# Two attentions of a two-layer transformer block, weighed with their values as the stationary operand

## The chip, the cores and the metric

The kernel runs on one core of one Trainium2 chip. The metric is the device time of one execution in microseconds (us). Engines are named as the profile names them: PE is the matrix engine (PEld its weight loads), DVE the vector engine, ACT the scalar engine, POOL is GpSimd, SP the queue that issues most of the DMA transfers. A matmul has a stationary operand, which is loaded into the array, and a moving operand, whose columns stream through.

## The reference, cut to what matters

256 tokens of width 1024 pass a first block (grouped attention "a" with 8 query and 2 key/value heads of 64, differential attention "b", output projection, MLP) and a second one (gated FFN, an mLSTM and a "forgetting attention" of 16 heads of 64 side by side, gated merge, output projection, a second gated FFN). The change is about attention a and the forgetting attention (fox), whose two halves of eight heads are called fx0 and fx1:

```python
s = jnp.einsum('bkgqd,bksd->bkgqs', qblk, kt).astype(jnp.float32) * scale      # attention a
p = jax.nn.softmax(s, axis=-1)
return jnp.einsum('bkgqs,bksd->bkgqd', p.astype(vt.dtype), vt)

logits = jnp.einsum('bhqd,bhkd->bhqk', q_blk, k).astype(f32) * scale + (F_blk[..., :, None] - F[..., None, :])
logits = jnp.where(k_pos[None, :] <= q_pos[:, None], logits, -jnp.inf)          # fox
p = jax.nn.softmax(logits, axis=-1)
return jnp.einsum('bhqk,bhkd->bhqd', p.astype(v.dtype), v)
```

All is float32. Attention a's output goes into rows 0 to 511 of `w_out`, the fox output into `w_branch_b`.

## The kernel before, in words

**Large products.** Each weight matrix is streamed from HBM in units of 2x128 rows by 512 columns. ACT copies a unit into a rounded high part (L1525), DVE subtracts it for the low part (L1907), and PE forms high*high, high*low and low*high (L1217, L1221, L1222) for each of two token tiles, into one of two pairs of PSUM banks. The activations are the stationary operand and have to be there transposed and split in the same way: a group of four 128x128 transposes on PE into one PSUM bank, a copy into the high part on ACT, a subtraction for the low part on DVE.

**Attention.** Each attention works on rounds `i` of two heads and one tile of 128 queries: eight rounds in attention a and in each fox half, the first four for one tile of queries, the last four for the other. Two rounds are scored together: `scores` (L1293) issues four matmuls on the upper and the lower 64 rows of the array in turn (L1312). `soft` takes the maximum on DVE and the exponential with its row sums on ACT (L1680, L1685). The transposing step `turn` (L1332) turns the probabilities with up to four PE transposes (L1338) into a bank, ACT or DVE copies them to `PT`, and `weigh` (L1342) multiplies: the turned probabilities are stationary (128x128), the values move, 64 columns (L1357). The key blocks number two in attention a and in rounds 0 to 3 of fox, one in rounds 4 to 7 of fox because of the causal mask. PE does a float32 matmul as two instructions, so a round of `weigh` is 8 instructions, or 4 with one key block. The result has queries in partitions and 8x64 columns. After four rounds DVE inverts the row sums (L2184) and multiplies the bank by them into W1 (L2198 for a, L2189 for fox). Since the next product needs it transposed, PE turns it again: jobs `ta0`, `ta1` (one group of four transposes each, L1391) and `yb0`, `yb1` (two groups each, L1270), followed by the split on ACT and DVE. `yb` also waits until branch a's product has read yTh and yTl, which it overwrites, and fox may not write W1 before `yT` has read it. Differential attention b has the same shape but works with 128-column values (L1372) and is not changed.

**Order.** A planner (`plan`, L434) writes one list of steps which all engines follow. Large products come in fixed order, and after each half unit `tick` advances small jobs whose lag has run out; the lags stand in the table `LAG`, with `PACED` for blocks that tick several times per half unit, `ADA` for the pace of the modulation weights and `LO` for how late the low part of a unit is made. The five blocks of the first projection come as qb, kb, vb, qa, ka. Then nothing large is left but the output projection, whose blocks `ob` need attention b's result, and `oa` attention a's. In the meantime PE has only the small steps of the attentions. In the second block the fox attention runs beside the products o, ga, ba and gb, and `bb` needs its result.

POOL computes powers of small statistics (L2502), masks (L2546, L2552) and multiplies the mLSTM's gain (L2538).

Of the kernel before, what the change touches and what calls it, by code (L numbers as in the profile page):

```python
# [16 lines left out]
OUTS = 2  # L17
# [4 lines left out]
LAG = {("attn", "sums"): 5, ("attn_a", "wait"): 21, ("attn_as", "round"): 4, ("attn_as", "wait"): 0,  # L22
       ("attn_as", 0): 6, ("attn_as", 1): 4, ("attn_as", 2): 3, ("attn_as", 3): 12, ("attn_at", "round"): 8,
       ("attn_at", 0): 4, ("attn_at", 1): 5, ("attn_at", 2): 3, ("attn_at", 3): 3, ("attn_at", 4): 1,
       ("attn_at", 5): 10, ("attn_at", 6): 1, ("attn_at", 7): 17, ("attn_aw", "round"): 3, ("attn_aw", 0): 4,
       ("attn_aw", 1): 3, ("attn_aw", 2): 8, ("attn_aw", 3): 1, ("attn_aw", 4): 7, ("attn_aw", 5): 4,
       ("attn_aw", 6): 1, ("attn_aw", 7): 17, ("attn_b", "wait"): 2, ("attn_bm", "round"): 10, ("attn_bm", 0): 2,
       ("attn_bm", 1): 1, ("attn_bm", 2): 2, ("attn_bm", 3): 4, ("attn_bs", "round"): 4, ("attn_bs", "wait"): 0,
       ("attn_bs", 0): 4, ("attn_bs", 1): 4, ("attn_bs", 2): 4, ("attn_bs", 3): 4, ("attn_bt", "round"): 5,
       ("attn_bt", 0): 1, ("attn_bt", 1): 6, ("attn_bt", 2): 7, ("attn_bt", 3): 1, ("attn_bw", "round"): 16,  # L30
       ("attn_bw", 0): 2, ("attn_bw", 1): 2, ("attn_bw", 2): 3, ("attn_bw", 3): 1, ("conv", 0): 3, ("conv", 1): 3,
       ("conv", 2): 4, ("end", "late"): 3, ("end", "lead"): 4, ("ffn1", "between0"): 0, ("ffn1", "between1"): 0,
# [3 lines left out]
       ("fox", 0): 1, ("fox", 1): 5, ("fox", 2): 8, ("fx0", "wait"): 7, ("fx0s", "round"): 11, ("fx0s", "wait"): 2,  # L36
# [21 lines left out]
ADA = {"attn": 0, "ffn1": 4, "ffn2": 7, "merged": 8, "mix": 11, "mixT": 0, "mlp": 3, "u_ffn1": 4, "u_ffn2": 6,  # L58
       "u_mlp": 3, "y": 4, "yb": 5}
LO = {"attn": 3, "begin": 5, "ffn1": 3, "ffn2": 3, "merged": 0, "mix": 3, "mixT": 3, "mlp": 3, "u_ffn1": 1,  # L60
      "u_ffn2": 0, "u_mlp": 3, "y": 2, "yb": 0}


class Dry:
# [80 lines left out]
def build(nc, d, out):  # L145
    f32 = mybir.dt.float32
# [2669 lines left out]
```

## Time and profile before

| what | value |
|---|---|
| median of 3 runs | 980.27 us (980.14 to 983.6) |
| profiled execution, its own time | 980.24 us |
| its span, first to last instruction | 978.9 us |
| PE busy | 963.1 us, 98% |
| DVE busy | 701.4 us, 72% |
| ACT busy | 523.0 us, 53% |
| POOL busy | 56.2 us, 6% |

The span lies 1.3 us below the execution's own time, and that time is the median to 0.03 us. Matmuls overlap, so that each one's own duration is longer than the distance to the next one's start. What PE pays for a piece of work is therefore read from the starts of what stands before and behind it.

### The profile page before, as it was taken

How to read it: one execution, taken by the hardware profiler on the slowest of the kernel's cores; microseconds unless marked ns; L12 is line 12 of the kernel's file. 1: busy time of each engine (PE TensorE's matmuls, PEld its weight loads, DVE VectorE, ACT ScalarE, POOL GpSimd, SP SyncE). 2: the span in 40 equal slices, each digit the busy share in tenths (PEclk: the TensorE clock that was granted, in tenths of full speed). 3: DMA queues.
4: the chain of work that ended last, by engine and by line, in shares of the span. 5: the costliest groups of instructions: out<-in, count | busy, mean ns of one | idle time of the engine just before them, and what ended most of it. 6: DMA issues, size and time to landing. Idle time of an engine off the chain costs nothing.

```text
span 978.9 us, 12466 instructions
## 1 busy us (share of the span) xinstructions
PE 963.1 (98%) x4614; PEld 792.9 (81%) x4614; DVE 701.4 (72%) x1045; ACT 523.0 (53%) x800; POOL 56.2 (6%) x62
## 2 busy tenths in 40 slices
PE   9988999999999999999999999999999999999998
PEld 7777888888888888888788888877888878888886
DVE  6787678987776676687669987578768764555553
ACT  7576665554446444443576565477554474444431
POOL 2311000000000000000000121121000000000000
PEclk9999999999999999999999999999999999999999
DMA  9641768887894888888747775865637535555561
GB/s 342 216 151 44 237 214 279 299 292 258 291 359 137 297 275 276 280 276 291 250 128 228 246 238 175 269 214 187 213 119 245 195 118 184 171 185 193 203 215 43
DMA packets 110122, 216.19 MB, mean 221 GB/s; under 512 B 8242, under 2 KB 15562, under 8 KB 109806
## 3 DMA queue, kind: packets, MB, share of 16 engines
q1 hardware_dynamic: 109918, 215.13, 65.5%
q8 instruction: 36, 0.59, 0.2%
q10 hardware_dynamic: 144, 0.27, 0.1%
q14 instruction: 24, 0.20, 0.1%
HBM read 214.29 MB, written 2.13 MB: 221 GB/s over the span
## 4 chain that ended last, share of the span: by engine, by line
PE 91%; DVE 3%; ACT 2%; DMA 2%; issue 1%; POOL 0%; SPq 0%; ACTq 0%; DVEq 0%; POOLq 0%
PE ps L1217 28%; PE ps L1222 27%; PE ps L1221 27%; PE ps L1270 3%; PE ps L1357 2%; PE ps L1312 1%; PE ps L1338 1%; DMA NF<-scr_g 1%; PE ps L1248 1%; ACT whi L1525 1%; DMA raw<-in_w_mix 1%; DVE wlo L1907 1%; DMA raw<-in_w_in 0%; DVE nat L1990 0%; DVE x L1994 0%
## 5 line engine op out<-in xcount | busy, mean ns | idle before, releaser
L1525 ACT ACTIVATE whi<-raw 128x1024 fp32r<-128x1024 f32 (+1 forms) x300 | 311.4, 1047 | 263.0 <-PE ps L1222 208.0
L1907 DVE TENSOR_TENSOR wlo<-raw,whi 128x1024 fp32r<-128x1024 f32 (+1 forms) x300 | 358.1, 1211 | 70.9 <-ACT whi L1525 70.3
L1217 PE MATMUL ps<-whi,hTh 128*128 128x512 f32 (+1 forms) x800 | 319.7, 400 | 1.1 <-ACT hTh L1537 1.1
L1221 PE MATMUL ps<-wlo,hTh 128*128 128x512 f32 (+1 forms) x800 | 311.1, 389 | 0.0
L1222 PE MATMUL ps<-whi,hTl 128*128 128x512 f32 (+1 forms) x800 | 311.0, 389 | 0.0
L1217 PEld LDWEIGHTS ps<-whi,hTh 128*128 128x128 f32 x800 | 150.8, 189 | 32.3 <-issue 2.2
L1222 PEld LDWEIGHTS ps<-whi,hTl 128*128 128x128 f32 x800 | 150.7, 188 | 32.0
L1221 PEld LDWEIGHTS ps<-wlo,hTh 128*128 128x128 f32 x800 | 150.9, 189 | 28.6 <-issue 0.4
L2502 POOL TENSOR_TENSOR stat<-stat,mhalf 128x8 f32<-128x8 f32 (+3 forms) x29 | 36.2, 1259 | 606.0 <-DVE stat L1923 485.8
L1217 PE MATMUL ps<-whi,uh_ffn 128*128 128x512 f32 x176 | 69.2, 393 | 0.0
L1222 PE MATMUL ps<-whi,ul_ffn 128*128 128x512 f32 x176 | 68.6, 390 | 0.0
L1221 PE MATMUL ps<-wlo,uh_ffn 128*128 128x512 f32 x176 | 68.6, 390 | 0.0
L1911 DVE TENSOR_TENSOR ul_ffn<-ps,uh_ffn 128x512 fp32r<-128x512 f32 x22 | 15.2, 691 | 70.5 <-ACT uh_ffn L1627 70.5
L2247 DVE CUSTOM_DVE_ANT_0 araw<-araw,crow,colp 128x1024 f32<-128x1024 f32 x48 | 61.3, 1278 | 0.8 <-DMA araw<-in_w_mod 0.6
L1217 PE MATMUL ps<-whi,uh 128*128 128x512 f32 x128 | 50.3, 393 | 0.0
L1222 PE MATMUL ps<-whi,ul 128*128 128x512 f32 x128 | 49.9, 390 | 0.0
L1221 PE MATMUL ps<-wlo,uh 128*128 128x512 f32 x128 | 49.9, 389 | 0.0
L1222 PEld LDWEIGHTS ps<-whi,ul_ffn 128*128 128x128 f32 x176 | 33.0, 188 | 7.0
L1221 PEld LDWEIGHTS ps<-wlo,uh_ffn 128*128 128x128 f32 x176 | 33.1, 188 | 6.7
L1217 PEld LDWEIGHTS ps<-whi,uh_ffn 128*128 128x128 f32 x176 | 33.1, 188 | 6.7
L2263 DVE SCALAR_TENSOR_TENSOR gate<-araw,cs,gate 128x512 f32<-128x512 f32 x42 | 32.4, 771 | 1.6 <-DMA araw<-in_w_ada 0.8
L1270 PE MATMUL ps<-ident,nat 128*128 128x128 f32 x208 | 31.1, 272 | 2.5 <-DVE nat L2089 1.4
(256 smaller groups left out, 1074.3 us busy)
## 6 DMA issues: line engine op xcount, KB each, us to landing
raw<-in_ffn_w_in SPq DMA_DIRECT2D x80, 512.0 KB, 4.6
raw<-in_w_mix SPq DMA_DIRECT2D x64, 512.0 KB, 4.5
araw<-in_w_mod SPq DMA_DIRECT2D x48, 512.0 KB, 5.3
raw<-in_ffn_w_out SPq DMA_DIRECT2D x44, 512.0 KB, 4.2
raw<-in_w_up SPq DMA_DIRECT2D x32, 512.0 KB, 5.2
raw<-in_w_down SPq DMA_DIRECT2D x32, 512.0 KB, 5.6
araw<-in_w_ada SPq DMA_DIRECT2D x24, 512.0 KB, 4.9
raw<-in_w_out SPq DMA_DIRECT2D x16, 512.0 KB, 3.8
```

What stands on the lines that cost most here:

```text
L1217: pe.e.matmul(o, ah, h[:, j, :], start=s0, stop=False, skip_group_check=True)
L1221: pe.e.matmul(o, ah, l[:, j, :], start=False, stop=False, skip_group_check=True)
L1222: r = pe.e.matmul(o, al, h[:, j, :], start=False, stop=s1, skip_group_check=True)
L1248: r = pe.e.transpose(bank[:, c * 128:(c + 1) * 128], src[:, (4 * p + c) * 128:(4 * p + c + 1) * 128], ident[:, :])
L1270: r = pe.e.transpose(bank[:, c * 256 + t * 128:c * 256 + t * 128 + 128], src[t][:, (2 * p + c) * 128:(2 * p + c + 1) * 128], ident[:, :])
L1357: r = pe.e.matmul(ob[:, h * 64:(h + 1) * 64], buf[:, (nk * c + k) * 128:(nk * c + k + 1) * 128], (fV if a["fox"] else VA)[:, k, v0:v0 + 64 ...
L1525: act.e.activation(uflat(whi, u), uflat(raw, u), ACT.Copy).then_inc(hi.up(u), 1)
L1907: v.tensor_tensor(uflat(wlo, u), uflat(raw, u), uflat(whi, u).bitcast(f32), SUB).then_inc(lo_dve.up(u), 1)
L1911: v.tensor_tensor(o, bank, h.bitcast(f32), SUB).then_inc(lower.up(name, p), 1)
L2247: v.tensor_tensor_reduce(out=w, in0=w, in1=crow[:, :], scale=1.0, scalar=col("bada", 8 * m + i), op0=MUL, op1=ADD, accum_out=modc[:, 8 * m ...
L2263: r = v.scalar_tensor_tensor(acc, buf[:, k, :], cs[:, kt:kt + 1], acc, MUL, ADD)
L2502: g.tensor_tensor(o, a, mhalf[:, 0:n], ALU.pow).then_inc(rstd.up(*key), 1)
```

## The change

- `weigh` of attention a and fox swaps its operands: the values (128x64) are stationary and the turned probabilities (128 columns) move. The two heads of a round go to partitions 0 to 63 and 64 to 127 of the same bank, in turn, and round `i` takes columns `128*(i%4)` on. The bank then holds the output already transposed. The heads come in another order, for which the rows of `w_out` and `w_branch_b` are permuted on the host.
- The jobs' transposes `ta0`, `ta1`, `yb0`, `yb1`, the DVE multiplications L2189 and L2198 and their reciprocals go. ACT and DVE split the bank directly, for fox into new tensors ybTh and ybTl.
- Since queries are now in the free dimension, the probabilities are divided before they are turned: DVE inverts four sums per pair of rounds, GpSimd multiplies in place (four instructions per pair), and `turn` waits for that.
- The block qa comes before vb. All tables of lags are new; qb is paced too, `ob0` from 2 to 6 ticks and `ob1` from 5 to 25.

```diff
-    for key, c0, n in (("qb", 768, 512), ("kb", 1280, 512), ("vb", 1792, 512), ("qa", 0, 512), ("ka", 512, 256)):
+    for key, c0, n in (("qb", 768, 512), ("kb", 1280, 512), ("qa", 0, 512), ("vb", 1792, 512), ("ka", 512, 256)):
...
-                pe.wait_ge(*(p_mix(i) if name == "attn_b" else p_exp(name, i)))
+                pe.wait_ge(*(p_mix(i) if name == "attn_b" else p_norm(name, i)))
...
-                for c in range(2):
-                    h = head_of(i, c)
-                    for k in range(nk):
-                        v0 = a["half"] * 512 + h * 64 if a["fox"] else hq // 2 * 64
-                        r = pe.e.matmul(ob[:, h * 64:(h + 1) * 64], buf[:, (nk * c + k) * 128:(nk * c + k + 1) * 128],
-                                        (fV if a["fox"] else VA)[:, k, v0:v0 + 64], start=(k == 0), stop=(k == nk - 1))
+                for k in range(nk):
+                    for c in range(2):
+                        v0 = a["half"] * 512 + head_of(i, c) * 64 if a["fox"] else hq // 2 * 64
+                        r = pe.e.matmul(ob[64 * c:64 * c + 64, hq * 128:(hq + 1) * 128],
+                                        (fV if a["fox"] else VA)[:, k, v0:v0 + 64],
+                                        buf[:, (nk * c + k) * 128:(nk * c + k + 1) * 128], start=(k == 0), stop=(k == nk - 1))
...
-            jobs[f"ta{t}"] = turn_tile(f"ta{t}", t, mixed_a(t))
...
+        def upper_out(name, of, b, dst):
+            act.wait_ge(*weighed(of, 4 * b + 3))
+            act.e.activation(dst, heads(misc.buf(of, "o", b)[:, :], 4), ACT.Copy).then_inc(upper.up(name), 1)
...
+                    qt, h = a["qt"](2 * k), 4 * (k % 2)
+                    dve.wait_ge(*p_exp(name, 2 * k + 1))
+                    v.reciprocal(st(8, name, "r", qt)[:, h:h + 4], st(8, name, "s", qt)[:, h:h + 4]).then_inc(
+                        p_root.up(name, k), 1)
...
+        def lower_out(name, of, b, h, l):
+            dve.wait_ge(*upper(name))
+            v.tensor_tensor(l, heads(misc.buf(of, "o", b)[:, :], 4), h.bitcast(f32), SUB).then_inc(lower.up(name), 1)
+            misc.give(lower(name), of, "o", b)
...
+        def normalize(name, k):
+            a = attention(name)
+            qt = a["qt"](2 * k)
+            w, r = (qt + 1) * 128 if a["fox"] else 256, st(8, name, "r", qt)
+            pool.wait_ge(*p_root(name, k))
+            for i in (2 * k, 2 * k + 1):
+                for c in range(2):
+                    o, h = a["P"].buf(name, i)[:, c * w:(c + 1) * w], head_of(i, c)
+                    z = g.tensor_scalar(o, o, r[:, h:h + 1], None, MUL)
+                z.then_inc(p_norm.up(name, i), 1)
```

## Rows read from the trace of the kernel before

**Rows 1.** The page: busy time by engine, and the chain that ended last.
```profile
PE 963.1 (98%) x4614; PEld 792.9 (81%) x4614; DVE 701.4 (72%) x1045; ACT 523.0 (53%) x800; POOL 56.2 (6%) x62
...
PE 91%; DVE 3%; ACT 2%; DMA 2%; issue 1%; POOL 0%; SPq 0%; ACTq 0%; DVEq 0%; POOLq 0%
```

**Rows 2.** Busy time in stretches: us, PE, PEld, DVE, ACT, POOL, clock, DMA share, GB/s.
```profile
140.00:240.00 100.00, 100.00 (x473) 82.73 (x472) 83.90 (x107) 54.25 (x65) 0.00 (x0) 1.00 0.82 280
...
68.20:90.90 22.70, 17.57 (x132) 14.81 (x132) 18.54 (x47) 12.96 (x39) 3.38 (x4) 0.92 0.14 48
...
79.00:81.00 2.00, 1.90 (x10) 1.13 (x6) 1.77 (x5) 0.92 (x3) 0.00 (x0) 0.50 0.01 4
...
675.00:700.00 25.00, 23.65 (x126) 19.32 (x125) 18.65 (x32) 13.95 (x24) 0.00 (x0) 1.00 0.52 161
```

**Rows 3.** PE's timeline around one group of transposes: start, us, line, count.
```profile
228.26 0.39 PE L1221 MATMUL ps<-wlo,uh 128*128 128x512 f32 x1
228.49 0.40 PE L1222 MATMUL ps<-whi,ul 128*128 128x512 f32 x1
228.73 0.60 PE L1270 MATMUL ps<-ident,nat 128*128 128x128 f32 x4
...
229.40 0.40 PE L1221 MATMUL ps<-wlo,uh 128*128 128x512 f32 x1
```

**Rows 4.** PE's timeline, rounds of `weigh` with two key blocks and with one.
```profile
89.73 1.00 PE L1357 MATMUL ps<-VA,PT 128*128 128x64 f32 x8
90.57 0.60 PE L1338 MATMUL ps<-ident,P 128*128 128x128 f32 x4
...
722.46 0.56 PE L1357 MATMUL ps<-fV,fPT 128*128 128x64 f32 x4
722.85 0.39 PE L1338 MATMUL ps<-ident,fP 128*128 128x128 f32 x2
```

**Rows 5.** PE's timeline: attention b's round, and pairs of scores on array halves.
```profile
63.16 1.06 PE L1372 MATMUL ps<-VB,PT 128*128 128x128 f32 x8
63.98 0.36 PE L1217 MATMUL ps<-whi,hTh 128*128 128x256 f32 x1
...
87.28 1.13 PE L1312 MATMUL ps<-kaT,qaT 64*128 64x256 f32 x8
88.35 1.10 PE L1357 MATMUL ps<-VA,PT 128*128 128x64 f32 x8
...
651.82 0.40 PE L1222 MATMUL ps<-whi,hTl 128*128 128x512 f32 x1
652.14 0.71 PE L1312 MATMUL ps<-fkT,fqT 64*128 64x128 f32 x8
652.79 0.66 PE L1357 MATMUL ps<-fV,fPT 128*128 128x64 f32 x4
```

**Rows 6.** ACT's timeline: the last copy out of ka's bank.
```profile
68.75 0.40 ACT L1650 ACTIVATE VA<-ps,stat 128x128 f32<-128x128 f32 x1
```

**Rows 7.** DVE's timeline: low parts, ka's first sum, ka's last step, a reciprocal.
```profile
69.46 2.35 DVE L1907 TENSOR_TENSOR wlo<-raw,whi 128x1024 fp32r<-128x1024 f32 x2
...
72.57 0.27 DVE L2036 TENSOR_REDUCE stat<-sq 128x2 f32<-128x128 f32 x1
...
75.35 0.89 DVE L2098 TENSOR_TENSOR kd<-nat,stat 128x128 f32<-128x128 f32 x4
76.16 0.19 DVE L2184 RECIPROCAL stat<-stat 128x8 f32<-128x8 f32 x1
```

**Rows 8.** Groups of POOL's instructions, nearest in shape to the new ones.
```profile
L2538 POOL TENSOR_TENSOR nat<-nat,row 128x512 f32<-128x512 f32 x4 | 5.2, 1331 | 14.9 <-ACT nat L1839 14.9
L2546 POOL TENSOR_SCALAR_AFFINE_SELECT NF<-NF 128x1024 f32<-128x1024 f32 x2 | 3.2, 1591 | 16.3 <-DMA NF<-scr_g 16.3
...
L2566 POOL MEMSET ones<- 128x256 f32 x1 | 0.3, 312 | 0.0
```

**Rows 9.** The DVE group that multiplies the fox output, removed by the change.
```profile
L2189 DVE TENSOR_TENSOR W<-ps,stat 128x512 f32<-128x512 f32 x4 | 2.8, 691 | 0.1
```

More of the change, by code:

```diff
@@ L228, in build @@
     sM = ExitStack()
+    sQ = ExitStack()
+    ybTh = sb("ybTh", [128, 8, 256], f32r, c=sQ)
+    ybTl = sb("ybTl", [128, 8, 256], f32r, c=sQ)
+    sQ.close()
     fqT = sb("fqT", [128, 8, 256], c=sM)
@@ L688, in job_scores @@
                     yield lag(f"{name}m", k, lag(f"{name}m", "round", 2))
+                else:
+                    yield lag(f"{name}n", k, 2)
+                    seg(f"{name}s")
+                    done.update({(name, 2 * k), (name, 2 * k + 1)})
+                    yield lag(f"{name}s", k, lag(f"{name}s", "round", 4))
         def job_weigh(name, P, PT, n, ready, more=None):
@@ L706, in job_weigh @@
                     b, last = (i - 1) // (n // 2), i % (n // 2) == 0
-                    while (i - 1) % (n // 2) == 0 and outs() >= OUTS or last and name == "fx0" and "yT" not in done:
+                    while (i - 1) % (n // 2) == 0 and outs() >= OUTS:
                         yield 1
@@ L726, in job_sub, with job_split @@
             yield from turn_segments(f"tb{t}", 1, kind)
-        def job_ta(t):
-            yield lag("ta", "wait", 1)
-            yield from turn_segments(f"ta{t}", 1, "ta")
+        def job_split(name, of, b):
+            yield lag(name[:2], "wait", 1)
+            misc.drop(of, "o", b)
+            seg(name)
+            yield 1
         def resid(stage, key, c, gate, t):
@@ L981, in job_yT @@
             yield from turn_segments("yT", 4, "yT")
-        def job_ybT(half):
-            while f"fx{half}" not in done:
-                yield 1
-            yield lag("yb", "wait", 1)
-            yield from turn_segments(f"yb{half}", 2, "yb")
         def job_mT(name):
@@ L1155, in turn_sources @@
             return [W1[:, t, :] for t in range(2)]
-        if name[:2] == "yb":
-            a = 512 * int(name[2])
-            return [W1[:, t, a:a + 512] for t in range(2)]
         a = 512 * int(name[2])
@@ L1857, in scalar_program @@
         for t in range(2):
-            jobs[f"ta{t}"], jobs[f"tb{t}"] = upper_tile(f"ta{t}", t), upper_tile(f"tb{t}", t)
+            ts = slice(t * 128, (t + 1) * 128)
+            jobs[f"tb{t}"] = upper_tile(f"tb{t}", t)
+            jobs[f"ta{t}"] = upper_out(f"ta{t}", "attn_a", t, mixTh[:, 0:4, ts])
+            for f in range(2):
+                jobs[f"yb{f}{t}"] = upper_out(f"yb{f}{t}", f"fx{f}", 1 - t, ybTh[:, 4 * f:4 * f + 4, ts])
         for c in range(8):
@@ L2455, in vector_program @@
         for t in range(2):
-            jobs[f"ta{t}"], jobs[f"tb{t}"] = lower_tile(f"ta{t}", t), lower_tile(f"tb{t}", t)
+            ts = slice(t * 128, (t + 1) * 128)
+            jobs[f"tb{t}"] = lower_tile(f"tb{t}", t)
+            jobs[f"ta{t}"] = lower_out(f"ta{t}", "attn_a", t, mixTh[:, 0:4, ts], mixTl[:, 0:4, ts])
+            for f in range(2):
+                c = slice(4 * f, 4 * f + 4)
+                jobs[f"yb{f}{t}"] = lower_out(f"yb{f}{t}", f"fx{f}", 1 - t, ybTh[:, c, ts], ybTl[:, c, ts])
         for c in range(8):
@@ L2804 @@
     w_mod = np.stack([np.asarray(inputs["w_ada_2"])[0, :, m * D:(m + 1) * D].T for m in (0, 1, 3, 4, 6, 7)])
+    pairs = np.array([64 * (2 * (j - j % 2 + c) + j % 2) + np.arange(64) for j in range(4) for c in range(2)]).ravel()
+    w = np.array(data["w_out"])
+    w[0, 0:512] = data["w_out"][0, pairs]
+    wb = np.array(data["w_branch_b"])
+    wb[0] = data["w_branch_b"][0, np.concatenate([pairs, 512 + pairs])]
+    data.update(w_out=w, w_branch_b=wb)
     data.update(w_mod=np.ascontiguousarray(w_mod), colp=np.ascontiguousarray(colp), w_gate=w_gate,
```

160 lines of the change are left out of this document (75 added, 85 removed), and 28 rows, old and new, of the table LAG.

## The prediction

> **What bounds the kernel now.** I read the page first, then busy time by stretches, then PE's timeline. The page shows PE busy for 98% of the span and the last-ending chain 91% on PE [rows 1]. By stretches, PE is busy for all of 140 to 240 us, and in most other places too; DVE stands at 84% even there [rows 2]. So over nearly the whole span an instruction less on PE is time gained, and a shorter chain elsewhere is worth nothing. The largest exception is 68.2 to 90.9 us, between ka's product and the first `ob` product: PE is busy for 17.57 of 22.7 us, and the granted clock averages 0.92, with 0.50 (the 1.2 GHz level) at 79 to 81 us, after idle stretches [rows 2]. Idle costs 5.1 us, the clock some 0.08 x 22.7 = 1.8: 6.9 us to be had, and here chains count. The wait before branch a's product is the other one I name: 1.35 us idle between 675 and 700 us [rows 2].
>
> **Transposes removed.** Around a group of four transposes, products that start 0.23 us apart (228.26, 228.49) would have put the second one behind at 228.95; it starts at 229.40 [rows 3]. A group costs 0.45 us. The change removes ta0, ta1 and four groups of yb: 6 x 0.45 = **2.7 us**, all on PE and in stretches where PE is full or the chain waits. Adjacent groups share the cost of switching, so 2.1 is the lower bound.
>
> **Weighing, PE.** A round with two key blocks takes 90.57 - 89.73 = 0.84 us, one with a single block 0.39 [rows 4]. There are 8 + 2x4 = 16 of the first and 8 of the second: 13.4 + 3.1 = 16.5 us. After the change a round has as many instructions, but 128 columns move instead of 64. Attention b's round has 8 instructions with 128 moving columns and takes 0.82 [rows 5], about 0.10 us each, the same as with 64. So if the two column halves of the array worked one after the other, the swap alone would be free and would bring nothing. The trace has no pair on column halves. The nearest rows are the scores on row halves: 8 instructions of 128 columns take 0.65, those of 256 columns 1.07 [rows 5]. Doubling the columns adds 0.42, so the fixed part is 0.23, and the rest is 0.42 for 8 instructions of 128 columns: half of attention b's 0.82. Halves do run side by side there. The fixed part is what a change of the array's division costs, and before it the last product's distance is 0.32 instead of 0.23 [rows 5], 0.09 more.
>
> If column halves behave like row halves, a long round costs 0.42 + 0.32 = 0.74 and a short one 0.21 + 0.32 = 0.53. That is 16 x 0.10 saved and 8 x 0.14 lost, 0.5 us saved. Where rounds stand back to back the switch is paid once, so I take 0.27 instead of 0.32: 16 x 0.15 - 8 x 0.09 = 1.7, and between the two **1.0 us saved**. The bounds: no switch at all, 16 x 0.42 + 8 x 0.18 = 8.2 us saved; halves one after the other with the full switch, 0.82 + 0.32 = 1.14 and 0.41 + 0.32 = 0.73, which is 16 x 0.30 + 8 x 0.34 = 7.5 us lost.
>
> That a change of division has a price agrees with the Trainium skill, which says that changing the tiling mode drains the engine (TensorEngine Tiling (Array Packing), Key Properties). Another of its rules speaks against this change: loads overlap running matmuls only when the row group differs (TensorE: Matmul & The Clock Gate, Part 3), and two column halves share all rows; by it the weighing would tend to the serial bound and the sum would come out 8.5 us higher. The same page reports a speed-up of 2.38 for three column tiles, measured; no run here shows either.
>
> **The stretch after ka.** ka's bank is copied out by 69.15 us [rows 6], but DVE first finishes qa's rotation and makes two low parts, 2.35 us, and takes up ka's sums only at 72.57. From there to the end of `kd` at 76.24 is 3.7 us [rows 7]. With qa ahead of vb, its rotation lies beside vb's product. Then ka could be taken up at 69.2, 3.4 us earlier, or 1.0 us earlier if the low parts stay in front. The scores, and all of attention a, move with it. In addition `ob` is spread more thinly between attention a's rounds (6 and 25 ticks), so that products fill waits. I take **4.0 us** of the 6.9, the 3.4 plus a part of the clock's loss; the bounds are 0 and 6.9. DVE is busy for 18.54 of the 22.7 us [rows 2], so this is its stretch as much as PE's; six multiplications of 0.69 go in all [rows 9], two of them here (by the diff, a's are of the same shape).
>
> **Dividing, a new wait.** `turn` waits for a reciprocal (0.19 for eight columns [rows 7]) and for POOL. POOL's 128x1024 mask takes 1.59, so 0.40 per 256 columns; a memset of 128x256 0.31; a product of two tensors of 128x512 1.33, so 0.67 per 256 [rows 8]. I take 0.40, nearest in kind as it reads one tensor. A pair of rounds in attention a is 1.6 us, the first round of it 0.8. It adds 0.2 + 0.8 = **1.0 us** where it is exposed, once, before the first round of attention a. Later pairs and all of fox have products on PE in front. Bounds: hidden, 0; exposed at each of four pairs with 0.67, 4 x (0.2 + 1.3) = 6 us. POOL's total grows by 16 x 0.40 + 2 x 4 x (0.40 + 0.20) x 2 = 16 us on 56; nobody else waits for it except small powers and masks, queued behind it by up to 1.6 us, which fox hides. If that cover is gone, each pair costs the same 1.0.
>
> **At no cost.** Splitting replaces splitting one for one on ACT and DVE. Six DVE multiplications of 0.69 go, off the path outside the stretch. DMA issues do not change in number; vb's and qa's units swap places. The separate ybTh and the removed wait for yT free jobs but remove no PE work; the wait at 675 us is for mLSTM's output, so I leave 1.35 there. The other new lags I set to nothing, plus or minus 1.5 us.
>
> **Sum.** -2.7 - 1.0 - 4.0 + 1.0 = -6.7, from 980.24 to **973.5 us**. The profiled execution equals the median within 0.03 us, so it holds for that as well.
>
> **Rivals.**
> 1. Column halves work one after the other. For it: no row shows them side by side, while attention b's rows give 0.10 per instruction regardless. Against: row halves do. Weighing loses 7.5 instead of winning 1.0: 973.5 + 8.5 = 982.0 us. Chance 0.12.
> 2. The stretch after ka stays as long: something else becomes late, for instance the low parts of `ob` on DVE, or vb, which now arrives late for attention b and so for `ob`. For it: DVE is 82% busy there. Against: attention b's rounds come at 63 us and later, behind vb's new place. 973.5 + 4.0 = 977.5. Chance 0.12.
> 3. Slower: dividing on POOL becomes what paces attention a, at 78 to 100 us. Each pair waits for exponential, reciprocal and four POOL instructions; the price is the 6 us instead of 1, with no gain from the stretch (4) and the short rounds at the full switch (1): 973.5 + 5 + 4 + 1 = 983.5, and with the clock staying at the lower level for another 3 us of work, 985 and above. It decides once POOL's instruction exceeds 0.67 us and less than 1.5 us of products stand between pairs. Chance 0.08; together with 1 it is 990.
> 4. Better: no price for the switch, and the stretch filled. 980.24 - 2.7 - 8.2 - 6.9 + 1.0 = 963.4; with half of each excess 968.5. Chance 0.13.
> 5. The forecast, 973.5: 0.55.
>
> A difference of 0.5% (4.9 us) is about what a measurement can tell from none here: below 975.3 is faster, above 985.1 slower. Of the forecast's 0.55 I put 0.46 below 975.3; the better case adds 0.13, the second rival 0.02: **0.61 faster**. Slower takes 0.06 of the third and 0.02 of the first: **0.08**. The rest, **0.31**, is no difference. The range from **965.5 to 982.0** reaches half way into the better case and takes in rivals 1 and 2; outside lie some 0.1 at either end together with the extremes.
>
> **What would show it.** Right: 24 transposes fewer; a long round of L1357's successor at some 0.7 us from its start to that of the next group and matmul starts in pairs; `kd` finished near 73 us; PE busy for more than 19.5 us of the 22 after ka's product, without a stretch at clock 0.5; POOL near 72 us. Wrong: a long round at 1.1 us (rival 1), `kd` still near 76 us (rival 2), PE idle before the turning of attention a with POOL as releaser, several times (rival 3). My forecast falls if PE's busy time stays within 3 us of 963 with the stretch unchanged.

## The result, and the profile after

The changed kernel takes **984.89 us** (median of 20 runs, 982.95 to 986.53) against 982.23 for the kernel before (20 runs). The ratio is 1.0024, with an interval of 1.0012 to 1.0035. It is slower by 0.24%, less than the 0.5% that the prediction counted as a difference. The measured time lies above the forecast of 973.5 and above its range, which ended at 982.0. The profiled execution took 985.87 us, with a span of 984.5 and a mean clock of 0.991 (before 978.9 and 0.998).

The two profiles exaggerate the difference. That of the kernel before shows one of its quicker executions (980.24 us, 2 below the median, and the base of the forecast), that of the changed kernel one of its longer ones. The executions of one kernel differ with their mean granted clock: in its 92 executions beside the experiments the kernel before took 981.0 us on average at 0.998 (35 of them) and 985.2 at 0.995 (13), and the changed kernel took 984.1 at 0.995 (10 of its 20, none higher).

The page after, busy time by engine and the chain that ended last, as in [rows 1]:

```profile
PE 962.5 (98%) x4590; PEld 784.6 (80%) x4590; DVE 702.2 (71%) x1045; ACT 523.1 (53%) x800; POOL 105.1 (11%) x110
...
PE 87%; DVE 5%; ACT 2%; issue 2%; DMA 2%; POOL 2%; SPq 0%; ACTq 0%; DVEq 0%; POOLq 0%
```

Twenty-four matrix instructions are gone, as the prediction said. PE's share of the chain fell from 91 to 87%, and DVE's rose from 3 to 5%: the new time is waiting. POOL is busy for 105.1 us where about 72 was forecast. DVE's busy time did not fall: six multiplications of 0.69 us are gone and six more reciprocals came, but why the total stays at 702 us isn't shown.

The stretches after, in the columns of [rows 2]:

```profile
68.20:90.90 22.70, 16.60 (x113) 12.47 (x112) 17.27 (x54) 14.69 (x45) 9.74 (x11) 0.85 0.20 66
...
75.00:81.00 6.00, 5.56 (x23) 4.07 (x24) 4.25 (x12) 2.14 (x4) 1.01 (x1) 0.50 0.01 3
...
648.00:651.00 3.00, 3.00 (x12) 1.52 (x10) 0.93 (x1) 1.89 (x2) 3.00 (x3) 0.50 0.45 124
...
675.00:700.00 25.00, 22.53 (x127) 16.95 (x126) 14.47 (x34) 14.82 (x32) 6.47 (x8) 0.86 0.39 132
...
682.00:688.00 6.00, 5.25 (x27) 3.96 (x28) 1.71 (x3) 1.34 (x3) 2.82 (x5) 0.50 0.00 0
```

The stretch after ka was to be filled; it became emptier (16.60 instead of 17.57 us busy) and its clock fell from 0.92 to 0.85. Ahead of branch a's product, 675 to 700 us, the idle time grew from 1.35 to 2.47 us, and the clock fell from 1.00 to 0.86. The kernel before had one stretch at a granted clock of 0.50 after its start, 3.4 us from 78.4 us on. In this execution of the changed kernel there are three, with 17.0 us together: 6.8 from 74.3, 3.4 from 647.7 and 6.8 from 681.9.

PE's longest waits after. The columns are the engine and line, what it waited for, us in total, times, and the longest one:

```profile
PE ps L1337 <- POOL fP L2553: 4.6, 2, 2.5
PE ps L1270 <- DVE kd L2101: 3.4, 1, 3.4
PE ps L1337 <- POOL P L2553: 2.4, 2, 1.5
```

PE waits for the division on POOL four times, 7.0 us in all; the larger part lies in fox, where I had counted on products as cover. The wait for `kd` is single and longer than the 1.19 of the kernel before. Two more waits came with the new order of blocks, where PE had none before: from 40 to 60 us it is idle for 2.1 us, 0.66 for kb (`kbT`) and 1.48 for qa (`nat`). The new instructions, by shape (busy us, mean ns of one), and those of fox by minimum, median and maximum of their durations in ns:

```profile
L2553 POOL TENSOR_SCALAR fP<-fP,stat 128x256 f32<-128x256 f32 x16 | 18.9, 1194 | 18.4 <-DVE stat L2164 18.4
L2553 POOL TENSOR_SCALAR P<-P,stat 128x256 f32<-128x256 f32 x16 | 15.7, 999 | 4.2 <-DVE stat L2164 4.2
L2553 POOL TENSOR_SCALAR fP<-fP,stat 128x128 f32<-128x128 f32 x16 | 14.2, 901 | 22.4 <-DVE stat L2164 22.4
...
L2553 POOL TENSOR_SCALAR fP<-fP,stat x32: 597/922/2495, 643.6 to 730.5; 128x256 f32<-128x256 f32 x16, 128x128 f32<-128x128 f32 x16
```

An instruction of 128x256 takes 1.0 to 1.2 us on average. The averages are raised by single long ones: in attention a the median is 0.93 us, and the quickest of 128x128 in fox take 0.60. I had taken 0.40 for 128x256, with 0.67 as the bound. POOL's 48 instructions take 48.8 us, and this is the growth from 56.2 to 105.1.

PE's timeline after, in the columns of [rows 3], with attention a's first turning, two rounds in one group, a long round, a short one and the drain of fox:

```profile
85.07 0.66 PE L1337 MATMUL ps<-ident,P 128*128 128x128 f32 x4 [1.48 <-POOL P L2553]
...
104.97 1.09 PE L1355 MATMUL ps<-PT,VA 128*64 128x128 f32 x16
...
656.81 0.40 PE L1222 MATMUL ps<-whi,hTl 128*128 128x512 f32 x1
657.14 0.66 PE L1355 MATMUL ps<-fPT,fV 128*64 128x128 f32 x8
657.72 0.50 PE L1217 MATMUL ps<-whi,hTh 128*128 128x512 f32 x1
658.06 0.39 PE L1221 MATMUL ps<-wlo,hTh 128*128 128x512 f32 x1
...
679.25 0.44 PE L1355 MATMUL ps<-fPT,fV 128*64 128x128 f32 x4
679.62 0.66 PE L1270 MATMUL ps<-ident,W 128*128 128x128 f32 x4
682.75 0.66 PE L1337 MATMUL ps<-ident,fP 128*128 128x128 f32 x2 [2.47 <-POOL fP L2553]
```

The same place of a round between two products in the kernel before:

```profile
659.50 0.39 PE L1222 MATMUL ps<-whi,hTl 128*128 128x512 f32 x1
659.73 1.00 PE L1357 MATMUL ps<-fV,fPT 128*128 128x64 f32 x8
660.54 0.48 PE L1217 MATMUL ps<-whi,hTh 128*128 128x512 f32 x1
660.85 0.39 PE L1221 MATMUL ps<-wlo,hTh 128*128 128x512 f32 x1
```

Before, a product, the round and the next product start 0.23 and 0.81 us apart; after, 0.33 and 0.58. So a long round is 0.23 us shorter, and switching the array costs 0.10 in front of it: 0.13 net. A short round takes 0.37 (0.39 before, [rows 4]), so with the switch it loses 0.08. Leaving the halves costs little: the product behind the round takes 0.34 to the next start instead of 0.31. My estimate from these rows is 16 x 0.13 - 8 x 0.08 = 1.4 us gained on PE, and somewhat less with the leaving.

And the stretch after ka on DVE: attention b's bias, a low part, ka's first sum, ka's last step:

```profile
68.93 1.22 DVE L1910 TENSOR_TENSOR wlo<-raw,whi 128x1024 fp32r<-128x1024 f32 x1
...
70.06 0.42 DVE L2130 CUSTOM_DVE_ANT_0 PA<-ps,biasT 128x256 f32<-128x256 f32 x1
...
71.44 0.28 DVE L2039 TENSOR_REDUCE stat<-sq 128x2 f32<-128x128 f32 x1
...
74.23 0.89 DVE L2101 TENSOR_TENSOR kd<-nat,stat 128x128 f32<-128x128 f32 x4
```

`kd` ends at 75.12 instead of 76.24, 1.1 us earlier where I had put 3.4. DVE itself is one reason: it runs without a pause here, and attention b's bias additions, the last at 71.09, stand in front of ka's first sum at 71.44. ACT is late as well. Its timeline after shows attention b's transposed probabilities, two high parts, and only then the copies out of ka's bank:

```profile
67.06 0.58 ACT L1705 ACTIVATE PT<-ps 128x512 f32<-128x512 f32 x1
67.54 2.00 ACT L1522 ACTIVATE whi<-raw 128x1024 fp32r<-128x1024 f32 x2
69.43 0.59 ACT L1705 ACTIVATE PT<-ps 128x512 f32<-128x512 f32 x1
...
70.79 0.39 ACT L1647 ACTIVATE VA<-ps,stat 128x128 f32<-128x128 f32 x1
```

ka's last bank leaves at 71.18 us, where it left at 69.15 before [rows 6], although ka's last product starts at 67.60 and before at 67.96. qa's rotation and one of the two low parts no longer stand in front of ka's sums on DVE, as forecast, but attention b, which now comes beside ka, stands in front of them on DVE and on ACT. ka's first squares are there at 70.33 us, 1.1 before DVE takes them up, so DVE's order decides.

### The profile page after: what moved, and what is told of

Its sections match the earlier page's. It is cut to its first block, busy times and chain, and to the rows that moved or that the text cites. A ratio compares the mean times of both kernels' runs of the same rounds, so it can differ in the third digit from the quotient of the medians.

```text
span 984.5 us, 12473 instructions
## 1 busy us (share of the span) xinstructions
PE 962.5 (98%) x4590; PEld 784.6 (80%) x4590; DVE 702.2 (71%) x1045; ACT 523.1 (53%) x800; POOL 105.1 (11%) x110
## 4 chain that ended last, share of the span: by engine, by line
PE 87%; DVE 5%; ACT 2%; issue 2%; DMA 2%; POOL 2%; SPq 0%; ACTq 0%; DVEq 0%; POOLq 0%
PE ps L1217 27%; PE ps L1221 26%; PE ps L1222 26%; PE ps L1270 3%; PE ps L1337 1%; DVE wlo L1910 1%; PE ps L1355 1%; POOL fP L2553 1%; DMA NF<-scr_g 1%; PE ps L1248 1%; PE ps L1312 1%; ACT whi L1522 1%; DMA raw<-in_ffn_w_in 0%; DMA raw<-in_w_in 0%; ACT P L1677 0%
## 5 line engine op out<-in xcount | busy, mean ns | idle before, releaser
L2553 POOL TENSOR_SCALAR fP<-fP,stat 128x256 f32<-128x256 f32 (+1 forms) x32 | 33.1, 1048 | 40.8 <-DVE stat L2164 40.8
```

Source lines behind the costliest of these rows:

```text
L2553: z = g.tensor_scalar(o, o, r[:, h:h + 1], None, MUL)
```

## The experiments

### Where the division costs, and whose theory holds

Theory A: the division costs what it makes PE wait for (my rival 3). Theory B: the new tables and the new order lose. Theory C: PE's own work hardly shrank, because the swapped weighing loses (rival 1) or gains too little. Five runs cut the change along these lines. In the second and the fifth the probabilities stay undivided, so both leave the division out.

```diff
 # e1, DVE divides, right behind its own reciprocal; POOL's part returns at once
+dve.wait_ge(*p_root(name, k))
+for i in (2 * k, 2 * k + 1):
+    for c in range(2):
+        o, hh = P.buf(name, i)[:, c * w:(c + 1) * w], head_of(i, c)
+        z = v.tensor_scalar(o, o, st(8, name, "r", qt)[:, hh:hh + 1], None, MUL)
 # e2, nobody divides
-pe.wait_ge(*(p_mix(i) if name == "attn_b" else p_norm(name, i)))
+pe.wait_ge(*(p_mix(i) if name == "attn_b" else p_exp(name, i)))
 # e3, the changed kernel with LAG, PACED, ADA, LO and the block order of before
 # e4, the kernel before with LAG, PACED, ADA, LO and the block order of after
-("vb", 1792, 512), ("qa", 0, 512), ("ka", 512, 256)
+("qa", 0, 512), ("vb", 1792, 512), ("ka", 512, 256)
 # e5, e2 with the block order, lags and paces of before in the first stage alone
```

> The changed kernel with the division of the probabilities on DVE, right behind its reciprocal, instead of on GpSimd; all else as changed. Theory A (GpSimd's four instructions of 0.92 us per pair are what PE waits for, 7.0 us of its idle time, and these waits bring on two of the three half-clock stretches, 10.2 us long in all, which cost half their length): the waits at 82 to 87, 644 to 647 and 680 to 683 us go, and the time is 972 to 977 us where the kernel before takes 982. Theory B (the new lags and the new order of blocks cost the time, through the waits for kb, qa and kd at 50 to 75 us): it stays within 2 us of the changed kernel, 983 to 985. Theory C (PE's own work hardly shrank): 980 to 982.

> The changed kernel without the division of the probabilities at all (left out: dividing by the row sums in attention a and fox), PE's turning step waits for the exponential. Theory A: 970 to 975 us, at most 3 us less than with the division on DVE. Theory B: 982 to 984. If the division on DVE is slow in its own way, this one is faster than that one by over 4 us.

> The changed kernel with the tables of lags and the order of blocks of the kernel before. Theory A: GpSimd's waits stay or grow, since the old lags leave less between exponential and turning: 980 to 988 us. Theory B: the stretch from 40 to 91 us is as before, and the saving on PE shows: 973 to 977 us.

> The kernel before with the tables of lags, the pacing and the order of blocks of the changed one, and nothing else. Theory A: within 3 us of before, 979 to 985. Theory B: the new order costs by itself 5 to 10 us: 987 to 992, with PE idle for some 5 us at 50 to 76 us.

> The kernel without the division (left out: dividing by the row sums in attention a and fox), but with the block order and the lags of the kernel before in the first stage (projection, attentions a and b, output projection); from the MLP on the tables of the changed kernel. If the new order costs the first stage some 3 us by its waits for kb, qa and kd, the second group of turns ahead of the MLP starts at 117 to 119.5 us (122.3 with the new order, 121.3 in the kernel before), and the time is 973 to 975 us. If the new order is as good as the old one once the division is gone, the group starts at 121 to 124 us and the time is 977 to 980.

| run | median us | ratio to before, interval | mean clock |
|---|---|---|---|
| changed kernel | 984.89 | 1.0024 [1.0012, 1.0035] | 0.991 |
| e1, DVE divides | 984.26 | 1.0018 [1.0002, 1.0034] | 0.993 |
| e2, no division | 977.73 | 0.9951 [0.9934, 0.9967] | 0.997 |
| e3, change with old tables | 1015.64 | 1.0346 [1.0322, 1.0369] | 0.976 |
| e4, before with new tables | 1001.49 | 1.0204 [1.0181, 1.0226] | 0.986 |
| e5, old first stage, no division | 979.85 | 0.9959 [0.9942, 0.9976] | 0.997 |

The mean clock in these tables is that of the profiled execution. The kernel before took 982.51 us in these groups. **Dividing costs 984.89 - 977.73 = 7.2 us**, and without it the change gains 4.8. So theory A holds for the sign, and C falls: the weighing with values stationary is in e2 too. The sizes were not foreseen: theory A had put e2 at 970 to 975 us and e1 at 972 to 977 (e1 came out where theory B had it), and e3 and e4 lie outside both of their ranges. Only the last sentence on e2 came true: it is faster than e1 by over 4 us.

A faster engine doesn't buy the time back: on DVE the same instruction takes a third of the time, less than the 0.40 us of the forecast, and the kernel takes only 0.6 us less, which the two intervals don't tell from nothing. Dividing on DVE still costs 984.26 - 977.73 = 6.5 us. Where each engine pays shows in the profiled executions, cut at the second group of transposes ahead of the MLP and at the first product of branch a:

| profiled execution | to the MLP's transposes | from there to branch a's product | rest |
|---|---|---|---|
| kernel before | 121.3 | 555.9 | 301.6 |
| e2, no division | 122.3 | 558.5 | 296.3 |
| changed kernel, POOL divides | 124.1 | 564.0 | 296.4 |
| e1, DVE divides | 126.0 | 560.1 | 296.4 |
| e8 (below), ACT divides | 124.7 | 562.4 | 297.5 |
| e5, old first stage, no division | 125.1 | 557.6 | 296.3 |

Their starts in the kernel before, in e2 and in the changed kernel:

```profile
121.32 1.03 PE L1248 MATMUL ps<-ident,x 128*128 128x128 f32 x8
...
677.26 0.48 PE L1217 MATMUL ps<-whi,yTh 128*128 128x512 f32 x1
```
```profile
122.31 1.03 PE L1248 MATMUL ps<-ident,x 128*128 128x128 f32 x8
...
680.77 0.52 PE L1217 MATMUL ps<-whi,yTh 128*128 128x512 f32 x1
```
```profile
124.11 1.04 PE L1248 MATMUL ps<-ident,x 128*128 128x128 f32 x8
...
688.12 0.74 PE L1217 MATMUL ps<-whi,yTh 128*128 128x512 f32 x1
```

Against e2, POOL's division costs 1.8 us in the first stage, where attention a is, 5.6 in the second, where fox's first half fx0 is divided (643.6 to 683.8 us in the changed kernel), and 0.1 in the rest, where fx1 is. DVE's costs 3.7, 1.6 and 0.1. The price goes with what else the engine and PE have to do there, and not with the duration of the instruction alone. These are single executions, and a stretch of 3.4 us at half clock more or less is up to 1.7 us of such a difference.

e1's instruction, and two of PE's waits in e1:

```profile
L2171 DVE TENSOR_SCALAR P<-P,stat 128x256 f32<-128x256 f32 x16 | 4.6, 348 | 0.1
```
```profile
PE ps L1337 <- DVE fP L2171: 2.9, 2, 1.9
...
PE ps L1390 <- DVE W L2054: 2.1, 1, 2.1
```

POOL's division is gone from the list, and DVE is late instead: 2.9 us with the division itself. The 2.1 for the rows `W` is little more than the 1.6 of e2, which doesn't divide.

The tables belong to the structure. In e3 PE waits for POOL three times as long as in the changed kernel, and with the new lags on the old structure it waits 5.4 us for fox's transposed probabilities and 3.8 for `W`. e3's and e4's waits:

```profile
PE ps L1337 <- POOL fP L2553: 15.5, 3, 8.3
PE ps L1337 <- POOL P L2553: 8.0, 2, 5.4
```
```profile
PE ps L1270 <- DVE fPT L2169: 5.4, 1, 5.4
PE ps L1338 <- DVE W L2189: 3.8, 1, 3.8
```

So theory B, taken as "the tables lose", falls as well: with the new structure they are worth 31 us against the old ones. It also means that e3 and e4 can't price a part alone, and neither can e5: it sets the old first stage beside the new weighing. It tells what the new first stage is worth to the new structure, 979.85 - 977.73 = 2.1 us by the medians, 0.8 by the ratios, whose intervals overlap. What it is worth against the kernel before, which the forecast put at 4.0 us, is read from the table of stages: even without the division the first stage ends at 122.3 us instead of 121.3, with one stretch of 3.4 us at half clock in either. (e5's time is in its second range; its first stage ends at 125.1, outside both.) PE's wait for `kd`, in e2:

```profile
PE ps L1270 <- DVE kd L2101: 3.4, 1, 3.4
```

It is as long as in the changed kernel, so the division isn't its cause, and the 2.1 us of idle time from 40 to 60 us are in e2 as well. Both belong to the new order.

### The clock, and the order of the heads

The division's waits stand beside stretches at half clock. If the clock takes part of the 7.2 us, matmuls on constants in these waits must bring it back, though nothing that PE waits for comes earlier. They write into a bank that the real group overwrites.

```diff
 # e6, ahead of four waits of turn
+for _ in range({("attn_a", 0): 3, ("attn_a", 1): 2, ("fx0", 0): 5, ("fx0", 6): 5}.get((name, i), 0)):
+    pe.e.matmul(bank[:, 0:256], ones[:, 0:128], ones[:, 0:256], start=True, stop=True)
 pe.wait_ge(*p_norm(name, i))
 # and seven of the same ahead of ka's turning, before its wait
 # e7, one head's blocks, then the other's
-for k in range(nk):
-    for c in range(2):
+for c in range(2):
+    for k in range(nk):
 # e8, ACT divides
+z = act.e.activation(o, o, ACT.Copy, scale=st(8, name, "r", qt)[:, hh:hh + 1])
```

> The changed kernel with dummy matmuls of 128x256 on PE in its longest waits: seven ahead of the turning of ka, three and two ahead of rounds 0 and 1 of attention a, five each ahead of rounds 0 and 6 of fx0. They go into banks that PE overwrites afterwards. If the half-clock stretches (6.8, 3.4 and 6.8 us) follow from PE's idle time in these waits, they go or shrink and the time falls by 3 to 7 us, to 978 to 982. If they have another cause, they stay and the time is 985 to 987.

> The changed kernel, but the two key blocks of one head are multiplied first, then those of the other, so that neighbouring matmuls of a long round are on the same column half three times out of four. If the column halves work side by side only where neighbours alternate, a long round of weighing goes from 0.59 us to about 0.8 and the time grows by up to 3 us, to 986 to 988. If the gain is from something else than side-by-side work (fewer stationary columns to load), rounds stay at 0.59 and the time at 984 to 985.

> The changed kernel with the division on ACT, copies in place with a scale, behind DVE's reciprocal. An ACT copy of 128x256 takes about 0.4 us where GpSimd takes 0.92 and DVE is full in the first stage. Theory A (what counts is how long the dividing engine takes and what else it has to do): between the kernel without division (977.7) and the one with DVE (984.3): 979 to 982 us. If any division at this place costs the same because the chain of exponential, sum, reciprocal and division is what is exposed: 983 to 985.

| run | median us | ratio to before, interval | mean clock |
|---|---|---|---|
| e6, filler matmuls | 981.95 | 0.9987 [0.9970, 1.0004] | 0.998 |
| e7, heads in turn | 984.73 | 1.0024 [1.0008, 1.0040] | 0.995 |
| e8, ACT divides | 986.23 | 1.0037 [1.0021, 1.0053] | 0.993 |

The fillers gain 984.89 - 981.95 = **2.9 us**. What PE waited for didn't come earlier: attention a's first turning starts at 85.15 us (85.07 in the changed kernel). Its row in e6, and e6's windows at the places where the changed kernel has its two long stretches at half clock:

```profile
85.15 0.66 PE L1343 MATMUL ps<-ident,P 128*128 128x128 f32 x4 [1.79 <-POOL P L2559]
```
```profile
75.00:81.00 6.00, 4.93 (x35) 3.30 (x34) 4.71 (x15) 2.06 (x4) 1.01 (x1) 1.00 0.02 5
...
682.00:688.00 6.00, 5.63 (x42) 4.04 (x43) 2.50 (x4) 3.12 (x5) 1.36 (x2) 1.00 0.00 0
```

Both are at the full clock with more instructions in the same 6 us (35 for 23, 42 for 27, of which a part are fillers). The time is at the upper end of the range for a clock that follows from the waits. Roughly 3 us of the changed kernel's time are thus the clock's. The share can't be laid on the division exactly: seven of the fillers stand in the wait for `kd`, which e2 has too, with a stretch of 3.4 us at half clock behind it, and no run has fillers without the division.

e7 asks how the weighing got shorter. My reason was that two halves of the array, with neighbouring instructions on either, work side by side. In the changed kernel a long round moves from one half to the other three times, in e7 once, and if that decided, its round should be longer. e7's timeline:

```profile
664.13 0.66 PE L1355 MATMUL ps<-fPT,fV 128*64 128x128 f32 x8
664.72 0.50 PE L1217 MATMUL ps<-whi,hTh 128*128 128x512 f32 x1
```

The round takes 0.59 us in either order (in the changed kernel 664.51 to 665.10), and the time of 984.73 us is as expected for that case, so alternating isn't what shortens it. What did change is what is loaded. The loads of the weighing, of the changed kernel and then of the kernel before, with their shortest, median and longest duration in ns:

```profile
L1355 PEld LDWEIGHTS ps<-PT,VA x64: 132/137/137, 88.7 to 105.7; 128*64 128x64 f32 x64
```
```profile
L1357 PEld LDWEIGHTS ps<-VA,PT x64: 186/192/192, 84.1 to 101.7; 128*128 128x128 f32 x64
```

64 stationary columns load in 137 ns, 128 in 192. The Trainium skill says that the load's time goes with the number of columns (TensorE: Matmul & The Clock Gate, the section on LDWEIGHTS); the rows agree in direction, 137 to 192 not being in the ratio of one to two.

What one more instruction costs is read from groups of different length. With values stationary, 4, 8 and 16 instructions last 0.44, 0.66 and 1.09 us: 0.054 each, plus a fixed part. That is close to what 128 moving columns take in the large products, which start 0.23 us apart with 512 (0.057 per 128). With probabilities stationary, 4 and 8 instructions last 0.56 and 1.00 us [rows 4], so 0.11 each with only 64 moving columns, and attention b's need about 0.10 with 128 [rows 5]. So the moving columns set the pace now, and something else did before. The load of 128 stationary columns fits, but no run varies it alone. No sign of halves at work at the same time is in these numbers, and none in the scores on row halves either: their 0.42 us for 128 more columns in eight instructions is 0.053 each, about the undivided array's pace.

By the Trainium skill's rule on row groups (TensorE: Matmul & The Clock Gate, Part 3), which the prediction set beside its serial bound, a long round would have come near 1.14 us with its switch; it takes 0.59, and 0.69 with the switch.

e8 adds the third engine: `activation` takes 0.496 us for 128x256, and PE then waits for ACT's copies of `fPT` (3.5 us) and for DVE's `mixTl` (2.3). The time, 986.23, is above both of its ranges. With e1 it says that the division costs 6.5 to 8.5 us at this place on any of the three engines, whether one instruction takes 0.35 or 1 us.

### Spreading fox and pacing the first stage

Between 675 and 690 us the changed kernel drains fox's rounds without products, since branch a's product needs `yT`. Theory D: with branch a's gates, output blocks and first blocks given out in portions, PE has work in the waits for POOL, and 3 to 4 us come back. Its rival: the products only change place, and what they move gets late.

```diff
 # e9
+# PACED gets "ga0", "ga1", "o1", "ba0"; ("pace", ...): 2; ("fx1s", "wait"): 1; ("fx1s", 2): 4
-drain("yT")
+while "yT" not in done:
+    for j in [j for j in jobs if j[2] in ("o0", "o1", "yT")]:
+        advance_job(j)
 # e10: ("pace", "qa"): 1 -> 3.  e11: e9 and e10.  e12: e11 and ("pace", "ka"): 1 -> 3
 # e15: e9 without o1 among the paced
```

> The changed kernel with GpSimd's division, and only the order in the fox stage changed: blocks o1, ga0, ga1 and ba0 tick twice per half unit, fx1's scores wait less, and ahead of branch a's product only yT's own steps are drained, so that no round of fox stands between products without one. If the division costs because of where it stands (rounds 3 to 7 of fx0 stand in that drain with nothing between them), the wait of 2.5 us at 680 us and the 6.8 us at half clock behind it go, and the time is 977 to 981 us. If GpSimd's 0.92 us per instruction cost the time wherever they stand, it is 983 to 986.

> The changed kernel with block qa ticking three times per half unit instead of once, so that kb is turned and attention b scored one block earlier, under vb's product instead of ka's; nothing else. If the new order costs time because attention b's scores and mixes stand on DVE ahead of ka's sums (71.4 us, 1.1 earlier than in the kernel before where I had counted on 3.4), kd ends near 72 us instead of 75.1, PE's waits for kb and kd (4.1 us) mostly go, and the time is 979 to 982. If DVE is merely full, the wait moves and the time stays at 984 to 985.

> Both of the previous edits together. If the two causes are apart, the gains add up: 973 to 978 us, which would be below the kernel before by over 0.4%. If the division's waits only move, 981 to 984.

> As the run before, with block ka ticking three times per half unit as well, so that attention b's weighing is mostly done under ka's product and the output projection's first blocks become ready earlier, as cover for attention a's chain with the division in it. If cover for that chain is what lacks, 2 to 3 us less than the run before: 971 to 976. If PE has then nothing left to do while it waits for ka, 2 us more than that run.

> The changed kernel, GpSimd's division, with ga0, ga1 and ba0 ticking twice, fx1's scores waiting less and only yT's steps drained ahead of branch a's product; the first turning of fox stays where it was. If the rounds of fx0 in that drain cost the time, the wait and the 6.8 us at half clock at 680 us go: 978 to 981 us. If denser rounds make other waits for GpSimd: 984 to 988.

| run | median us | ratio to before, interval | PE's longest waits |
|---|---|---|---|
| e9 | 991.99 | 1.0104 [1.0081, 1.0127] | POOL `fP` 8.2 |
| e10 | 987.99 | 1.0064 [1.0040, 1.0089] | DVE `nat` 3.2, `kd` 3.1 |
| e11 | 998.27 | 1.0162 [1.0135, 1.0189] | POOL `fP` 6.6, DVE `nat` 3.2, `kd` 3.1 |
| e12 | 1009.28 | 1.0269 [1.0243, 1.0294] | POOL `fP` 6.4, `P` 4.5, DVE `kd` 5.7 |
| e15 | 988.91 | 1.0073 [1.0046, 1.0099] | DVE `kd` 3.5, `yTl` 3.4, POOL 6.0 |

All five are slower than every range written for them. In e10 the wait for `kd` stays (3.1 us) and that for `nat` doubles (3.2 from 1.5): it moved, as the rival said, and cost more. e9, and with it e11 and e12, moved fox's first turning ahead of its mask's load, a mistake of the experiment: the wait of 8.2 us is the result, and these three say little on theory D. In e15 that was mended, and PE waits for `yTl`:

```profile
PE ps L1236 <- DVE yTl L1880: 3.4, 2, 2.4
```

In e15's profiled execution, its quickest with 987.26 us, the half clock near 682 us is gone, as theory D said, yet the kernel is 4 us slower than the changed one. `yT` gets late and is waited for, and POOL still is (6.0 us). Theory D falls in this form: the products given to the waits were ones that other work stood behind. I tried one distribution of each kind, so another may do better.

### A mixed version

e13 puts the division of each attention on the engine that costs less there by the table of stages (POOL in attention a, DVE in fox), with fillers as in e6, in part fewer. e14 asks whether two engines that divide at once do better.

```diff
 # e13: POOL divides for attention a, DVE for fox
+pe.wait_ge(*(p_mix(i) if name == "attn_b" else (p_halved if name != "attn_a" else p_norm)(name, i)))
+# fillers: {("attn_a", 0): 3, ("attn_a", 1): 2, ("fx0", 0): 2, ("fx0", 6): 4}, seven ahead of ka's turning
 # e14: even rounds on DVE, odd on POOL, fillers {("attn_a", 0): 1, ("attn_a", 1): 1, ("fx0", 6): 3}, seven
```

> The changed kernel with the division on GpSimd in attention a and on DVE in fox, and dummy matmuls in the waits (seven ahead of ka's turning, three and two in attention a's rounds 0 and 1, two and four in fx0's rounds 0 and 6). By the first stage of the filled kernel (123.7 us to the turns ahead of the MLP), the second of the one with DVE (670.1 us, less 1.7 for its half clock) and 186 us behind: 977 to 980 us, which would be under the kernel before. If the filling and the engine act on the same microseconds: 981 to 983.

> The changed kernel with the even round of each pair divided on DVE and the odd one on GpSimd at the same time, so that a pair is divided in 1.9 us instead of 3.7, and fillers as before (seven, one and one, three). If the duration of the division is what PE waits for: 976 to 980 us. If its place in the order decides: 981 to 984.

e13 took **980.38 us** against 982.32, a ratio of 0.9978 with an interval of 0.9962 to 0.9993. It beats the changed kernel (1.0012 to 1.0035) clearly, and the kernel before by 0.2%. In its profiled execution the two stages take 123.3 and 559.5 us, 1.0 more each than without the division. The 0.2% aren't the change's alone. e13's executions ran at a mean clock of 0.998 to 1.000, and the six of the kernel before that reached 1.000 took 980.3 us on average, the same. Fillers in the kernel before might bring it there too; no run tried that. Of e13's waits for the division one is left on PE, of 1.8 us in attention a. e14 took 982.58, a ratio of 1.0001 [0.9987, 1.0015], within its second range.

e14's instructions show what dividing on both engines costs:

```profile
L2571 POOL TENSOR_SCALAR fP<-fP,stat 128x256 f32<-128x256 f32 x8 | 10.8, 1361 | 18.4 <-DVE stat L2171 18.4
...
L2571 POOL TENSOR_SCALAR P<-P,stat 128x256 f32<-128x256 f32 x8 | 9.1, 1149 | 9.8 <-DVE stat L2171 9.8
...
L2180 DVE TENSOR_SCALAR P<-P,stat 128x256 f32<-128x256 f32 x8 | 3.4, 461 | 0.1
```

For 128x256 each slows the other: POOL from 0.999 to 1.149 us in attention a and from 1.194 to 1.361 in fox, DVE from 0.348 to 0.461. By the medians in attention a, which single long instructions don't move, POOL goes from 0.926 to 1.054. For 128x128 POOL's mean didn't rise (0.901 and 0.882).

## Why the prediction was wrong, by its own steps

The runs split the result as the sum did. Without the division the change gains 4.8 us (forecast 7.7), and the division costs 7.2 (forecast 1.0): -4.8 + 7.2 = +2.4, and the two medians differ by 2.7. The base was low too: 980.24 us for a kernel whose median over 20 runs is 982.2.

- **Dividing, a new wait: this step failed**, and with it the sign. I had it exposed once, before the first round of attention a, with products on PE in front of "later pairs and all of fox". It is exposed in attention a and in fx0: PE waits for POOL twice in attention a (2.4 us) and twice in fox (4.6), at 682.75 for instance, in the drain ahead of branch a's product, where my own row of the kernel before showed idle time. By the profiled executions the first stage pays 1.8 us and fx0's 5.6; behind branch a's first product, where fx1 is, products do cover it (0.1). The price of the instruction was wrong as well: I took 0.40 us from the mask, "nearest in kind as it reads one tensor", and bounded it with 0.67; it measured 1.0 to 1.2 on average. But this isn't what decided, for on DVE, with 0.35 us, the division still costs 6.5. What failed is the overlap that I assumed.
- **The stretch after ka: this step failed too.** Of the 4.0 us nothing shows. Without the division the first stage ends 1.0 us later than in the kernel before (122.3 and 121.3), though two groups of transposes are gone from it. `kd` ends 1.1 us earlier, not 3.4, since attention b stands on DVE and ACT where qa's rotation stood. And the text had nothing for the price of the new order: 2.1 us of idle time on PE from 40 to 60 us and a wait for `kd` of 3.4 instead of 1.2. My second rival named "something else becomes late", and it is this.
- **Weighing on PE: near in size, wrong in mechanism.** I took 1.0 us; the starts give an estimate of 1.4. But halves side by side aren't what does it, neither here (e7) nor in the rows of the scores from which I concluded it: an instruction takes there what its columns take in the undivided array. That the sum came out near is luck. "Halves one after the other with the full switch" did not come, as the round never came near 1.1 us.
- **Transposes: 24 instructions fewer**, as counted. No run has them alone. The lower bound's reason, that adjacent groups share the cost, isn't borne out: two groups behind each other in the kernel before start 0.44 us apart (86.31, 86.75), as much as one alone costs.
- **Where the 4.8 us without the division come from is open.** The medians give them; the two profiled executions differ by only 1.8 (spans of 978.9 and 977.1), since that of the kernel before is one of its quicker ones. In them the first stage is 1.0 longer, the second 2.5 longer and the rest 5.3 shorter, so that work has also changed its stage.
- **The clock** appears in my text as something won back (0.08 x 22.7 us). That a wait added on a full PE can bring a stretch at half clock with it was said only in rival 3. This rival named the engine, the place in attention a, and the signs (PE idle before the turnings with POOL as releaser, several times). Its price of 985 equals the result, but by luck: it laid 5 us on attention a, whose whole stage pays 1.8, and nothing on fox, where fx0's stage pays most. At 0.08 its chance was too small, since nothing in the trace had a POOL instruction of that kind, and both rows that I used were of another.

## What to carry to other kernels

- A new step in a chain costs where nothing covers it. Ask at each place whether products really stand between, above all where the code drains its jobs, and what else the engine has to do there: here POOL was the cheaper one in the first stage (1.8 us against 3.7) and DVE in the second (1.6 against 5.6).
- When work is moved to an engine that has not done this kind of instruction in the trace, its price is open upwards too.
- Tables of lags that are tuned for one structure can't be used to price a part of another: here the exchange cost 19 and 31 us.
- A wait on a full TensorE costs its length and, where the granted clock falls behind it, also the half speed of the work that follows. A few matmuls on constants in the waits took 2.9 us off here, though what PE waited for came no earlier.
- Which operand is stationary had a price of its own in these small f32 matmuls: 0.11 us for an instruction with 128 stationary columns, 0.054 with 64, and a tenth of a microsecond for the switch of the array's division before each round.

## What the runs showed of the hardware

- GpSimd's `tensor_scalar` in place, f32, with a scalar per partition, took 0.93 us for 128x256 (median in attention a of the changed kernel) and 0.60 for 128x128 (the four from 681.42 us on). The means are higher, 0.999 and 1.194 us for 128x256 and 0.901 for 128x128, as single instructions took up to 2.5. VectorE took 0.348 and 0.282, ScalarE's `activation` 0.496 and 0.389. If VectorE divides at the same time, both are slower for 128x256: GpSimd's mean by 15% and VectorE's by 32% (e14, attention a).
- A load of 64 stationary columns took 137 ns against 192 for 128.
- A turning group between two rounds on column halves took 0.58 us from its start to the next (89.30 to 89.88), against 0.44 before (89.29 to 89.73). 0.10 of it is the way into the next round, since a group with another group behind it took 0.49 (98.81 to 99.30). That a change of the tiling mode drains the engine is what the Trainium skill states (TensorEngine Tiling (Array Packing), Key Properties); the trace agrees, with 0.10 us before a round and 0.03 to 0.05 behind it.
